# Recurrent attention by one scan per pair over products copied to SBUF, in a new order of work, with twelve modulation groups in the dilated block

## The reference

```python
dS = jnp.einsum('bnshk,bnshv->bnhkv', k_end, vc)     # one 64 x 64 product for each chunk
decay = jnp.exp(b_last[:, :, 0])
def step(S_prev, inp):
    dec, ds = inp
    return dec[..., None] * S_prev + ds, S_prev
_, S_prevs = lax.scan(step, S0, (decay, dS))
o_inter = jnp.einsum('bnthk,bnhkv->bnthv', q_in, S_prevs)
return (o_intra + o_inter)
```

## Time and profile before

| | us |
|---|---|
| median of 3 runs (lowest to highest) | 2832.98 (2832.07 to 2837.13) |
| the profiled execution | 2837.96 |
| its span, first to last instruction | 2836.1 |
| TensorE busy | 2689.6 (95%) |
| VectorE, ScalarE, GpSimd busy | 1331.6, 992.9, 392.6 |

### The profile page before, as it was taken

One profiled execution on the slowest core, in us unless ns is written; L12 is line 12 of the kernel. 1 busy time (PEld: TensorE's weight loads), 2 busy tenths in 40 slices (PEclk: granted clock), 3 DMA queues, 4 the chain that ended last, 5 costly groups with the idle time before them and its releaser, 6 DMA issues. The chain is left out here.

```text
span 2836.1 us, 51236 instructions
## 1 busy us (share of the span) xinstructions
PE 2689.6 (95%) x21525; PEld 2077.8 (73%) x21525; DVE 1331.6 (47%) x2151; ACT 992.9 (35%) x1764; POOL 392.6 (14%) x334
## 2 busy tenths in 40 slices
PE   8988989999999999999999999999997888899998
PEld 7774664444444886666899999998886777788887
DVE  3224542323333514744576666664444554543445
ACT  4235331111111323255453333335374545433223
POOL 0005120000000401344100000000004564100000
PEclk9999999999999999999999999999999999999999
DMA  7527918999995212020112122212210000222232
GB/s 257 208 96 280 343 62 352 412 418 412 418 414 237 67 60 69 1 64 1 60 60 75 59 74 74 71 63 64 90 37 32 4 4 19 104 96 98 89 103 74
DMA packets 145227, 391.54 MB, mean 138 GB/s; under 512 B 17048, under 2 KB 75323, under 8 KB 132251
## 3 DMA queue, kind: packets, MB, share of 16 engines
q1 hardware_dynamic: 132810, 200.24, 20.7%
q10 hardware_dynamic: 12240, 188.75, 16.0%
HBM read 382.41 MB, written 5.77 MB: 137 GB/s over the span
## 5 line engine op out<-in xcount | busy, mean ns | idle before, releaser
L2431 PE MATMUL ps<-mlp_h_high,mlp_w_high 128*128 128x384 f32 (+2 forms) x512 | 171.9, 336 | 0.0
L2431 PE MATMUL ps<-mlp_h_high,mlp_w_low 128*128 128x384 f32 (+2 forms) x512 | 171.2, 334 | 0.0
L2431 PE MATMUL ps<-mlp_h_low,mlp_w_high 128*128 128x384 f32 (+2 forms) x512 | 171.1, 334 | 0.0
L2431 PE MATMUL ps<-mlp_x_high,mlp_w_high 128*128 128x384 f32 x456 | 153.4, 336 | 4.6 <-DVE mlp_x_low L2337 2.5
L2431 PE MATMUL ps<-mlp_x_high,mlp_w_low 128*128 128x384 f32 x456 | 152.4, 334 | 0.0
L2431 PE MATMUL ps<-mlp_x_low,mlp_w_high 128*128 128x384 f32 x456 | 152.4, 334 | 0.0
L2060 DVE TENSOR_TENSOR hT<-hT,ps 128x512 f32<-128x512 f32 x128 | 79.1, 678 | 92.5 <-PE ps L1886 92.5
L4070 PE MATMUL ps<-odd_x_high,conv_w_parts 128*128 128x512 f32 (+1 forms) x448 | 119.2, 354 | 0.0
L1891 PE MATMUL ps<-e_wg,aT 128*64 128x512 f32 x512 | 112.6, 592 | 2.6 <-DVE e_sel L2028 2.6
L1935 PE MATMUL ps<-ring,e_hidT 128*64 128x512 f32 x512 | 113.4, 595 | 0.0
L1891 PE MATMUL ps<-e_wu,aT 128*64 128x512 f32 x512 | 113.4, 595 | 0.0
(11 more groups left out here) (639 smaller groups left out, 6728.1 us busy)
## 6 DMA issues: line engine op xcount, KB each, us to landing
mlp_ring<-in_mlp_w_dram SPq DMA_DIRECT2D x64, 1024.0 KB, 5.1
e_wg<-in_w_gate_dram ACTq DMA_DIRECT2D x15, 4096.0 KB, 16.6
e_wu<-in_w_up_dram ACTq DMA_DIRECT2D x15, 4096.0 KB, 15.5
ring<-in_w_down_dram ACTq DMA_DIRECT2D x15, 4096.0 KB, 13.8
ring<-in_ada_w_dram SPq DMA_DIRECT2D x16, 2048.0 KB, 8.9
h_rest<-in_ada_w_dram SPq DMA_DIRECT2D x8, 2048.0 KB, 8.5
ring<-in_w_in_dram SPq DMA_DIRECT2D x6, 2048.0 KB, 10.5
proj_ring<-in_even_w_in_dram SPq DMA_DIRECT2D x8, 1024.0 KB, 5.2
```

The source lines that it names most:

```text
L2431: last = pe.matmul(out, wp, xp, start=start and i == 0, stop=stop and i == 2, skip_group_check=True)
```

## The change

The groups of the dilated block become twelve (8 to 19), behind units 1 to 6, 8 to 10 and 12 to 14; SyncE issues the fetches up to group 21 there, and four groups are left for the recurrent block. In that block the products of a pair are copied by ScalarE from PSUM to SBUF, four copies of 128 x 256, one for each bank, transposed on the way to the layout pair, value, chunk. GpSimd spreads the decay factors to the same layout, with chunk 0's set to zero. One scan over 1024 elements of each partition then makes all states of a pair (the zero decay restarts it at each value). The states are kept with the chunk innermost, so the outputs read a state with a step of 16 elements. The next products wait for the copies and not for the states. The attention norm comes later, the gate is multiplied before the norm factor, the table of ScalarE is loaded behind the copies, and the calls of each engine stand in a new order.

```diff
-FIRST, EARLY = 8, 16
+FIRST, EARLY = 8, 20
@@ dilated
-        multiplies = lambda u: u % 4 >= 2 if u < 4 else u % 4 < 2
-        group_of = lambda u: FIRST + 2 * (u // 4) + u % 2
+        MULTIPLIES = (1, 2, 3, 4, 5, 6, 8, 9, 10, 12, 13, 14)
+        multiplies = lambda u: u in MULTIPLIES
+        group_of = lambda u: FIRST + MULTIPLIES.index(u)
@@ hgrn
-    Sall = flat[:, 0:4 * 64 * NC].rearrange("p (j c v) -> p j c v", j=4, v=64)
+    Sall = flat[:, 0:4 * 64 * NC].rearrange("p (j v c) -> p j v c", j=4, v=64)
+        gained, fading = sb("hg_gained", [P, 4, 64, NC]), sb("hg_fading", [P, 4, 64, NC])
@@ TensorE
                 def attention_sums():
+                    pe.wait_ge(gains_out, 16)
...
-                    if j == 0:
-                        pe.wait_ge(arooted, 1)
-                    else:
-                        pe.wait_ge(states, j)
+                    if j:
+                        pe.wait_ge(gains_out, 4 * j)
...
                     elif j == 1:
-                        pe.wait_ge(states, 4)
+                        pe.wait_ge(gains_out, 16)
...
-                            last = pe.matmul(o(h2)[:, C * ch:C * ch + C], Sall[lo:lo + 64, j, ch - 1, :],
+                            last = pe.matmul(o(h2)[:, C * ch:C * ch + C], Sall[lo:lo + 64, j, :, ch - 1],
...
                 def sums(j):
...
-                        pe.wait_ge(states, 4)
+                        pe.wait_ge(arooted, 1)
...
                 turn_keys(0)
                 turn_keys(1)
                 turn_keys(2)
-                attention_sums()
-                modulate()
                 gain(0)
                 turn_keys(3)
                 scores(0)
-                modulate()
                 gain(1)
                 modulate()
                 gain(2)
+                gain(3)
                 scores(1)
-                modulate()
-                gain(3)
                 outputs(0)
+                attention_sums()
                 modulate()
                 scores(2)
                 outputs(1)
                 modulate()
+                scores(3)
+                outputs(2)
                 sums(0)
-                outputs(2)
-                scores(3)
+                sums(1)
                 modulate()
-                sums(1)
+                stream.fold(pe, 1)
+                outputs(3)
                 sums(2)
-                outputs(3)
-                modulate()
                 sums(3)
-                stream.fold(pe, 1)
                 constant_products(E, pe, 5, 8)
@@ ScalarE
-                act.preload_act_table_set("natural_log_exp_and_others")
+                def take_gains(j):
+                    act.wait_ge(gains, j + 1)
+                    for r in range(4):
+                        act.activation(gained[:, j, :, r:NC:4].rearrange("p v t -> p t v"), E.bank(r, 256).rearrange("p (t v) -> p t v", v=64),
+                                       ACT.Copy).then_inc(gains_out, 1)
+                copy_keys(0)
+                take_gains(0)
+                copy_keys(1)
+                copy_keys(2)
+                copy_keys(3)
+                take_gains(1)
                 for k in range(4):
                     act.activation(asq[:, k, :], H.attn[:, k, :], ACT.Square).then_inc(asquared, 1)
-                copy_keys(0)
-                copy_keys(1)
-                copy_keys(2)
+                take_gains(2)
+                take_gains(3)
+                act.preload_act_table_set("natural_log_exp_and_others")
+                take(0)
                 act.wait_ge(asummed, 1)
...             (the attention root, Ln and Exp, as before)
-                copy_keys(3)
-                take(0)
                 take(1)
+                take(2)
                 root(0)
-                take(2)
                 root(1)
+                stream.copy(act, 1)
+                take(3)
                 root(2)
-                take(3)
-                stream.copy(act, 1)
                 root(3)
@@ VectorE
                 def state(j):
-                    (the copy of chunk 0 and 14 steps)
+                    dve.wait_ge(gains_out, 4 * j + 4)
+                    dve.wait_ge(faded, j + 1)
+                    dve.tensor_tensor_scan(Sall[:, j].rearrange("p v c -> p (v c)"), fading[:, j].rearrange("p v c -> p (v c)"),
+                                           gained[:, j].rearrange("p v c -> p (v c)"), 0.0, ALU.mult, ALU.add).then_inc(states, 1)
...
                 def scale(j):
                     dve.wait_ge(rooted, 2 * j + 2)
+                    dve.wait_ge(opened, j + 1)
-                    dve.scalar_tensor_tensor(out=aT[:, 4 + j, 0:S], in0=oT[:, j, :], ...)
+                    dve.scalar_tensor_tensor(out=aT[:, 4 + j, 0:S], in0=aT[:, 4 + j, 0:S], ...)
...
-                state(0) masks(0) state(1) scale_attention(0, 2) state(2) masks(1) state(3) masks(2)
-                scale(0) masks(3) scale_attention(2, 4) scale(1) scale(2) scale(3) stream.finish(dve, 1)
+                for j in range(4):
+                    state(j)
+                    masks(j)
+                scale_attention(0, 4)
+                scale(0) scale(1) stream.finish(dve, 1) scale(2) scale(3)
@@ GpSimd
+                pool.memset(H.dec[:, :, 0:1], 0.0).then_inc(opening, 1)
+                pool.wait_ge(opening, 1)
                 for j in range(4):
-                    pool.wait_ge(scaled, j + 1)
-                    pool.tensor_tensor(aT[:, 4 + j, 0:S], aT[:, 4 + j, 0:S], H.gate[:, j, :], ALU.mult)
+                    pool.tensor_copy(fading[:, j], H.dec[:, j, :].unsqueeze(1).to_broadcast([P, 64, NC])).then_inc(faded, 1)
+                for j in range(4):
+                    pool.wait_ge(taken, j + 1)
+                    pool.tensor_tensor(aT[:, 4 + j, 0:S], oT[:, j, :], H.gate[:, j, :], ALU.mult).then_inc(opened, 1)
```

More of the change, by code:

```diff
@@ L1395, in hgrn @@
         sq, rstd, asq, arstd = sb("hg_sq", [P, 2, S]), sb("hg_rstd", [P, 2, S]), sb("dil_sq", [P, 4, S]), sb("dil_rstd", [P, S])
-        (cst_in, asquared, asummed, arooted, turned, keys_out, gains, state_steps, states, scored, masked, out, taken, squared,
-         summed, rooted, scaled) = (sem(f"hg_{x}") for x in (
-             "cst", "asquared", "asummed", "arooted", "turned", "keys_out", "gains", "state_steps", "states", "scored", "masked",
-             "out", "taken", "squared", "summed", "rooted", "scaled"))
+        gained, fading = sb("hg_gained", [P, 4, 64, NC]), sb("hg_fading", [P, 4, 64, NC])
+        (cst_in, asquared, asummed, arooted, turned, keys_out, gains, gains_out, opening, faded, states, scored, masked, out, taken, squared,
+         summed, rooted, opened) = (sem(f"hg_{x}") for x in (
+             "cst", "asquared", "asummed", "arooted", "turned", "keys_out", "gains", "gains_out", "opening", "faded", "states", "scored", "masked",
+             "out", "taken", "squared", "summed", "rooted", "opened"))
+        scaled = sem("hg_scaled")
         bank_k = lambda j: (4, 5, 6, 4)[j]
@@ L1567, in state @@
                 def state(j):
-                    gained = lambda ch: E.ps[:, ch % 4 * BANK + 64 * (ch // 4):ch % 4 * BANK + 64 * (ch // 4) + 64]
-                    dve.wait_ge(gains, j + 1)
-                    dve.tensor_copy(Sall[:, j, 0, :], gained(0)).then_inc(state_steps, 1)
-                    for ch in range(1, NC - 1):
-                        dve.wait_ge(state_steps, (NC - 2) * j + ch)
-                        ins = dve.scalar_tensor_tensor(out=Sall[:, j, ch, :], in0=Sall[:, j, ch - 1, :], scalar=H.dec[:, j, ch:ch + 1],
-                                                       in1=gained(ch), op0=ALU.mult, op1=ALU.add)
-                        ins.then_inc(state_steps if ch < NC - 2 else states, 1)
+                    dve.wait_ge(gains_out, 4 * j + 4)
+                    dve.wait_ge(faded, j + 1)
+                    dve.tensor_tensor_scan(Sall[:, j].rearrange("p v c -> p (v c)"), fading[:, j].rearrange("p v c -> p (v c)"),
+                                           gained[:, j].rearrange("p v c -> p (v c)"), 0.0, ALU.mult, ALU.add).then_inc(states, 1)
                 def masks(j):
@@ L1586, in scale @@
                     dve.wait_ge(rooted, 2 * j + 2)
-                    dve.scalar_tensor_tensor(out=aT[:, 4 + j, 0:S], in0=oT[:, j, :], scalar=E.v("hgrn_norm_g", j), in1=rstd[:, j % 2, :],
+                    dve.wait_ge(opened, j + 1)
+                    dve.scalar_tensor_tensor(out=aT[:, 4 + j, 0:S], in0=aT[:, 4 + j, 0:S], scalar=E.v("hgrn_norm_g", j), in1=rstd[:, j % 2, :],
                                              op0=ALU.mult, op1=ALU.mult).then_inc(scaled, 1)
@@ L1593, in scale_attention @@
                         dve.scalar_tensor_tensor(out=aT[:, k, 0:S], in0=H.attn[:, k, :], scalar=E.v("attn_norm_g", k), in1=arstd[:], op0=ALU.mult, op1=ALU.mult)
-                state(0)
-                masks(0)
-                state(1)
-                scale_attention(0, 2)
-                state(2)
-                masks(1)
-                state(3)
```

(17 more changed lines are left out.)

## The result

The changed kernel takes 2848.47 us in the median of 6 runs (2844.66 to 2850.58), the kernel before 2833.18 (6 runs, 2831.78 to 2837.13): ratio 1.0046, 95% interval 1.0035 to 1.0057, so 10 to 16 us slower. The forecast was 2835, its range ended at 2843. The profiled execution took 2849.48 us with a span of 2847.4, 11.3 us over that of before.

A forecast was written before the change was run, and what follows sets the result against it. TensorE's own order of work was taken to bound the recurrent block, transfers the dilated block's opening. +6.4 (dilated) and -4.4 (recurrent) made +2.0 us on the runs' median of 2832.98: 2835, range 2826 to 2843.

The forecast's parts named there:

- Dilated block, +6.4 forecast: Dilated block: with twelve groups for eight its last sums end at 277.1, not 270.7; floor +4.8, ceiling +10.
- a group starts when its unit's transposes are done and its weights are in: Dilated block: rule for group starts; it put group 12 at 235.0 and gave no size of its own.
- The walk: Step-by-step timing: dilated groups by three rules, sums at 277.1; recurrent block, 39.9 us of TensorE work plus 7.5 idle.
- weights land 7.7 us after their issue or 5.17 us after the group before: Dilated block: rule for landings of 2048 KB groups, whichever is later; groups 10, 13, 16 and 19 wait for weights.
- my ceiling's 10.9: Dilated block's upper end: 8.9 us landing per slot reuse, every second group 10.9 us apart, in all +10.
- Rival C: Dilated block holds the transfers badly: +10 in place of +6.4, time 2838.6 us; chance 0.10.
- Recurrent block, -4.4 forecast: Recurrent block: -4.9 to the last sums, -1.2 for the gate, +0.7 clock, +1.0 weight loads; 10 shorter to 5.5 longer.
- the size of a scattered weight load: Recurrent block: 240 state loads at a step of 16 elements, 4 ns more each, +1.0 us; ends 0 and +10.9.
- rival B: Recurrent block: each of 240 scattered loads 45 ns later, +10.9 us, time 2844.9; decides from about +19 ns; chance 0.14.
- TensorE's two waits for ScalarE: Recurrent block: TensorE idle for ScalarE's copies, 2.7 us before the scores, 0.4 before products 2, 3.5 before products 3.
- The forecast's case: Both blocks as forecast, +6.4 and -4.4, giving 2835 us, own range 2830 to 2840; chance 0.49.
- My own sign of being wrong: Dilated block growing by less than 4 or more than 10 us, or recurrent block not shrinking.

The follow-up runs named there:

- the copy early: Changed kernel with ScalarE's copy for the fold put in front of the pair's exponentials: 2844.43 us (9 runs), ratio 1.0046.
- half weights: Changed kernel with the fetches of groups 10 to 19 bringing 1 MB and not 2: 2839.05 us (11 runs).
- the dilated part only: Kernel before with twelve groups in the dilated block and four of eight group calls taken out of the old recurrent block: 2844.28 us (6 runs).

## Why the prediction was wrong

**Dilated block, +6.4 forecast, +15.3 measured** (+13.7 in the mean of the executions with the same code). Two steps failed. The first is the rule "a group starts when its unit's transposes are done and its weights are in". It knew nothing of the fold, which stands between group 11 and 12 and whose bank group 12 writes next. In the trace of before the fold waited 0.8 us and took 1.08, and I gave it no time; but it is bound to the unit of group 11, and moving that group from unit 5 to unit 4 put its copy behind the five activations that ScalarE does for a pair at that unit. Group 12 came 5.9 us late. With the copy early the way from group 10 to group 12 is 3.0 to 5.8 us shorter: 3.0 is the wait, which stands at 2.98 or 2.99 us in every execution with the late copy, and the rest a lower clock around it, which only the profiled execution of the change shows in full. The walk gave the clock a price at group 10 alone; over the block it cost 3.3 us more than before in the mean, 6.1 in that execution.

The second is "weights land 7.7 us after their issue or 5.17 us after the group before". By the real issue times it holds in the kernel after within 0.9 us; but once the copy is early four fetches in a row land after 10.1 to 10.4 us, up to 7.3 us behind the one before. With a slot free only after its multiplication, two groups then take 10.3 + 0.1 + 1.9 us or more, 1.4 us over my ceiling's 10.9. So the cost of the fold hides behind that of the weights: taken away alone, half weights bring 8.5 us of the block and the early copy nothing; behind half weights the copy brings 5.9 more. Why the landings differ between these kernels stays open. It is not that the stream is full: in two stretches beside such landings it ran at 142 and 194 GB/s.

**Rival C** had the block's transfers at +10 in place of +6.4. The block went beyond that, but in the kernel after mainly by the fold, of which C says nothing.

**Recurrent block, -4.4 forecast, -0.9 measured.** The step that failed is the size of a scattered weight load. I had 45 ns as the worst case and cut it to 4, arguing that an fp32 load is slow anyway and most of the surplus hidden. It is 26 ns exposed (64 ns more in the load itself), +6.2 us in place of +1.0. That is above the 19 ns from which **rival B** was to decide, with half its price. The Trainium skill ("Advanced Engine Details and Errata", section on SBUF cachelines) says that accesses each to another line of 16 bytes pay; the trace agrees, with 199 against 135 ns.

The other terms held: the scans 2.29 us (2.34 forecast), GpSimd's copies 1.04 (1.0 to 1.3), a set of four scattered copies 1.88 to 1.92 us (2.2), TensorE's two waits for ScalarE 2.32 and 2.06 (2.7, 0.4 and 3.5), the gate's 1.2: 1.1 between the last sums and M. TensorE is busy 46.8 us up to the last sums. With the 39.9 of the walk and 6.2 of loads that leaves 0.7, as much as I had allowed for the clock. Idle it is 5.5 us and not 7.5, which hid 2.0 us of the error. So the last sums come at 49.1 + 5.2 - 2.0 = T + 52.3; measured, T + 52.5.

**What the sum did not hold** is that a group is cover as well as work: while it runs, other engines get ahead, and TensorE keeps its clock. I wrote that taking four groups out of the recurrent block saves 7.7 us. With VectorE's steps kept it saved 2.1, as the waits for them grew from 3.0 to 7.3 us and the clock fell from 0.94 to 0.87. With the change's own order the waits that are left uncovered are ScalarE's.

**The chances.** The forecast's case had 0.49, B and C 0.14 and 0.10; the truth is B in part, and in the other block the fold, which no rival had. I treated B and C as alternatives, but they are mechanisms in two blocks and can both hold. Two small slips change nothing: the walk has group 10's weights in at 223.4, where 218.5 + 5.17 is 223.7, and the chance of faster is 0.18 by its own terms, not 0.20. My own sign of being wrong, a dilated block that grows by more than 10 us, came true.

## What to carry to other kernels

When a step is bound to a place ("behind the unit of group 11"), look up on every engine what else is done at the new place, not only what it waits for now. In a ring of two slots a late multiplication is a late fetch: a stall can hide behind the slow landings, as here, and look free until they are gone. Look at the busy time and the granted clock of a block beside its idle time: here the lower clock cost about as much as the added idle time (3.3 and 2.7 us in the mean). A layout that makes one instruction long and cheap (a scan) is paid for by whoever reads it: here 240 reads lost 26 ns each, for 60 instructions fewer on VectorE, for which TensorE had waited only 3.0 us.

## What the runs showed of the hardware

- A stationary fp32 operand of 64 x 64 with a step of 16 elements: 199 ns a load against 135 in line; 60 products that alternate halves of the array take 3.49 us against 1.94.
- VectorE's step on 64 elements read and written at that step takes 323 ns and not 281, ScalarE's copy of 256 from PSUM 625 and not 364.
- Landings of 2 MB in a steady stream were 7.5 to 7.8 us alone and up to 10.4 us with another fetch under way; 1 MB took 5.1 us in the median (half weights, groups 12 to 19).
- Behind a wait TensorE's work can be dearer: a group of sixteen matmuls took up to 3.64 us in place of 1.92, the fold 1.92 in place of 1.08. It isn't always so: with the copy early a group behind 2.36 us of waiting took 1.92. The same dilated block ran at a granted clock of 0.83 in the kernel after and 0.86 with the dilated part only, and TensorE was busy 70.1 and 67.0 us in it.
- A small fetch pays for the big one ahead: the mask of 64 KB, issued at 286.88 while group 21 was under way, landed after 5.6 us, 0.2 us behind that group; with the copy early it took 2.6 us and landed 0.2 us behind group 21 again, and in the kernel before, with nothing under way, 1.8. VectorE's first scan waited for it, 1.3 us longer than for its other inputs, at no cost to TensorE.
